# An output projection whose last slot hands over its two token halves one after the other

## The reference

```python
x = x + mixed @ w_out[l]                 # first block; then its mixture of experts
xn = rms_norm(x, ffn_norm[l])
...
h = h + mix                              # second block, layers 0 and 1; mix = o @ w_out
h = h + 0.5 * swiglu(rmsnorm(h, g[2]), ffn_w1[layer, 1], ffn_w3[layer, 1], ffn_w2[layer, 1])

def rmsnorm(x, g):
    xf = x.astype(F32)
    y = xf * lax.rsqrt(jnp.mean(xf * xf, axis=-1, keepdims=True) + EPS)
    return (y * g.astype(F32)).astype(x.dtype)
```

## Time and profile before

| | |
|---|---|
| median of 3 runs | 1673.91 us |
| the profiled execution's own time | 1673.79 us |
| its span in the trace | 1671.8 us |
| PE, DVE, ACT, POOL busy | 1554.4, 1140.2, 814.1, 42.5 us |
| mean granted clock of PE | 0.954 of full speed |

### The profile page before, as it was taken

How to read it: one execution, slowest core, us unless ns; L and a number is a source line. 1 busy time by engine, 2 the same in 40 slices (tenths; PEclk the granted TensorE clock), 3 DMA queues, 4 the chain that set the end, 5 groups by cost and what they waited for, 6 DMA issues and landing times.

```text
span 1671.8 us, 26989 instructions
## 1 busy us (share of the span) xinstructions
PE 1554.4 (93%) x9148; PEld 1352.5 (81%) x9148; DVE 1140.2 (68%) x1740; ACT 814.1 (49%) x1308; POOL 42.5 (3%) x53
## 2 busy tenths in 40 slices
PE   7898786999999989999996999999999999999997
PEld 6788674898898958888894788888788878888886
DVE  5845863798788947777544657777777765667775
ACT  6423442777677744444443453444444445654442
POOL 1120000000000000000000100000000000000000
PEclk9898787999999999999997599999999999999999
DMA  6312231799799947555451056556456544155552
GB/s 255 114 64 76 76 107 38 252 353 348 262 338 348 351 172 229 188 188 189 139 182 57 1 172 200 193 187 193 152 187 193 189 155 152 54 173 189 188 188 76
DMA packets 82148, 299.67 MB, mean 179 GB/s; under 512 B 9278, under 2 KB 9406, under 8 KB 81952
## 3 DMA queue, kind: packets, MB, share of 16 engines
q1 hardware_dynamic: 79632, 289.97, 51.6%
q0 software_dynamic: 2160, 8.66, 1.7%
q10 hardware_dynamic: 288, 0.12, 0.0%
HBM read 297.59 MB, written 1.11 MB: 179 GB/s over the span
## 4 chain that ended last, share of the span: by engine, by line
PE 85%; DVE 9%; ACT 4%; issue 1%; DMA 0%; POOL 0%; DVEq 0%; SPq 0%; POOLq 0%; ACTq 0%
PE ps L1680 17%; PE ps L1505 15%; PE ps L1506 14%; PE ps L1507 14%; PE ps L1678 10%; PE ps L1511 3%; PE ps L1677 2%; PE ps L1632 2%; DVE w_lo L921 2%; PE ps L1604 1%; PE ps L1697 1%; DVE xT L960 1%; PE ps L1772 1%; ACT arena L600 1%; ACT w_hi L545 1%
## 5 line engine op out<-in xcount | busy, mean ns | idle before, releaser
L921 DVE TENSOR_TENSOR w_lo<-raw,w_hi 128x1024 fp32r<-128x1024 f32 x549 | 653.4, 1221 | 230.7 <-ACT w_hi L545 229.5
L545 ACT ACTIVATE w_hi<-raw 128x1024 fp32r<-128x1024 f32 x549 | 549.1, 1055 | 337.6 <-PE ps L1507 306.4
L1680 PE MATMUL ps<-xT,w_hi 128*128 128x512 f32 x1232 | 439.6, 396 | 0.0
L1678 PE MATMUL ps<-xT,w_lo 128*128 128x256 f32 x1408 | 364.5, 279 | 0.0
L1678 PEld LDWEIGHTS ps<-xT,w_lo 128*128 128x128 f32 x1408 | 265.3, 188 | 16.1
L1680 PEld LDWEIGHTS ps<-xT,w_hi 128*128 128x128 f32 x1232 | 231.2, 188 | 47.1
L1505 PE MATMUL ps<-w_hi,xT 128*128 128x256 f32 (+2 forms) x848 | 261.6, 309 | 7.0 <-DVE w_lo L921 3.6
L1506 PE MATMUL ps<-w_lo,xT 128*128 128x256 f32 (+2 forms) x848 | 251.9, 297 | 0.0
L1507 PE MATMUL ps<-w_hi,xT 128*128 128x256 f32 (+2 forms) x848 | 251.8, 297 | 0.0
L1505 PE MATMUL ps<-w_hi,h_hi 128*128 128x512 f32 x480 | 188.4, 392 | 4.4 <-DVE h_lo L1121 4.4
L1506 PE MATMUL ps<-w_lo,h_hi 128*128 128x512 f32 x480 | 187.7, 391 | 0.0
(11 more groups left out here) (315 smaller groups left out, 1630.0 us busy)
## 6 DMA issues: line engine op xcount, KB each, us to landing
raw<-in_wstream SPq DMA_DIRECT2D x549, 512.0 KB, 5.0
arena<-bias_rows POOLq DMA_DIRECT2D x2, 2048.0 KB, 12.2
const<-in_const POOLq DMA_DIRECT2D x1, 1112.0 KB, 7.5
x_res<-in_x SPq DMA_DIRECT2D x2, 512.0 KB, 4.5
arena<-in_mem POOLq DMA_DIRECT2D x1, 1024.0 KB, 5.3
out<-arena SPq DMA_DIRECT2D x2, 512.0 KB, 2.7
smallw<-in_smallw POOLq DMA_DIRECT2D x1, 768.0 KB, 4.4
prow<-in_prow POOLq DMA_DIRECT2D x1, 512.0 KB, 5.1
```

Source lines behind the costliest of these rows:

```text
L545: nc.scalar.activation(w_hi[:, slot, lo:hi], raw[:, slot, lo:hi], ACT.Copy).then_inc(S_(f"hi_{part_}"), 1)
L921: tt(w_lo[:, slot, lo:hi], raw[:, slot, lo:hi], w_hi[:, slot, lo:hi].bitcast(F32), ALU.subtract).then_inc(S_(f"lo_{part_}"), 1)
L1678: low = mm(bank[:, 0:S], w_lo[:, s, c:c + P], xT_hi[:, k, :], start=False, stop=False)
L1680: last = mm(bank, w_hi[:, s, c:c + P], both, start=False, stop=k == KD - 1)
```

## The change

In the last slot of each of the three projections, the last matmul of token half 0 signals `half_psum`. DVE adds this half as soon as it comes, and signals `half_added`; ACT's Square of half 0 waits for that. Half 1 keeps its old signals. `RESIDUAL_ENDS` names the three slots that follow such a projection.

```diff
+RESIDUAL_ENDS = (MOE0, FFB0, FFD0)
...
                         if c:
-                            act.wait_ge(S_(wait[0]), wait[1] + t if wait[0] == "y_added" else wait[1])
+                            if wait[0] == "evacuated" and not t:
+                                act.wait_ge(S_("half_added"), RESIDUAL_ENDS.index(wait[2]) + 1)
+                            else:
+                                act.wait_ge(S_(wait[0]), wait[1] + t if wait[0] == "y_added" else wait[1])
...
-            norm(3, ("evacuated", evac_until(MOE0 - 1)))
+            norm(3, ("evacuated", evac_until(MOE0 - 1), MOE0))
...
                 if residual:
-                    dve.wait_ge(S_("d_used"), n + 1)
                     pair, n_first, places = psum_places(n)
                     w = len(places) * P
                     c = places[0][1][2]
                     for t in range(T):
+                        if n + 1 in RESIDUAL_ENDS and not t:
+                            end = RESIDUAL_ENDS.index(n + 1) + 1
+                            dve.wait_ge(S_("half_psum"), end)
+                        else:
+                            dve.wait_ge(S_("d_used"), n + 1)
                         ins = tt(x_res[:, t, c:c + w], ps[:, pair + t, 0:w], x_res[:, t, c:c + w], ALU.add)
+                        if n + 1 in RESIDUAL_ENDS and not t:
+                            ins.then_inc(S_("half_added"), 1)
                     ins.then_inc(S_("evacuated"), 1)
...
                         last = mm3(o, st, mv, k == 0, k == KD - 1)
+                    if not i and n + 1 in RESIDUAL_ENDS:
+                        last[2].then_inc(S_("half_psum"), 1)
```

More of the change, by code:

```diff
@@ L881, in _ @@
                 proj(n, evacuate=False)
-            norm(7, ("evacuated", evac_until(FFB0 - 1)))
+            norm(7, ("evacuated", evac_until(FFB0 - 1), FFB0))
             feed_forward(*ffs[2])
@@ L893, in _ @@
                 proj(n, evacuate=False)
-            norm(11, ("evacuated", evac_until(FFD0 - 1)))
+            norm(11, ("evacuated", evac_until(FFD0 - 1), FFD0))
             feed_forward(*ffs[4])
```

## The result

The changed kernel takes 1690.24 us (median of 4 runs, 1689.77 to 1691.09), the kernel before, run beside it, 1673.71 (4 runs, 1673.17 to 1674.88). The ratio is 1.0094 [1.0082, 1.0107]: 16.5 us slower. The forecast of 1669.7 us was wrong. What happened is the rival that I gave 0.04, and it is larger than I priced it. The profiled execution took 1691.09 us, its span 1689.1, and PE's mean granted clock is 0.935 (0.954 before).

What follows compares the result with a forecast made beforehand. PE was taken as the bound, except where it waits for the norms' serial chain. The profiled 1673.79 us less 4.21 gave 1669.6, and 0.1 for the median made 1669.7 us; range 1667.8 to 1672.8.

Steps and rivals of the forecast that it cites:

- the rival that I gave 0.04: Last attention, before place 3: falls to PE's lower clock; with 14 us fallen, +6.0 us net, 1679.9 us; chance 0.04.
- The sum: Norms behind the three projections: first add and first Square leave the chain, 1.41, 1.40 and 1.40 us, 4.21 in all.
- The signals and the read of the neighbouring bank: Three places: new PE signals taken as 0, at most 0.36 us; slower PSUM read 0, at most 0.1 each.
- The room to hide: Each place: hidden add and Square finish before the second Square is due, with 0.2, 0.2 and 0.25 us left.
- a shift's mean cost is nothing: Clock rise in the router's gather: monitor runs free of the program, so a shift has no side and costs nothing on average.
- The smaller rival: Router after place 1: clock rise stays while the gather comes earlier, 0.7 us lost, 1670.4; case put at 1671.3; chance 0.10.
- the clock's gain: Router's gather after place 1: an earlier clock rise gives back half of 3.0 us, 1668.2 us; chance 0.08.

Runs made afterwards that it cites:

- Runs 9 to 11: Useless matmuls ahead of the last attention: six in the changed kernel, 1673.01 us; nine in the kernel before, 1694.6; fifteen in the kernel before, 1678.2.
- run 5: Kernel before with the new signals at place 2 alone (FFB0): median 1690.88 us, ratio 1.0072.
- run 6: Kernel before with the new signals at place 1 alone (MOE0): 1674.08 us, ratio 0.9999.
- run 1: The changed kernel timed again, unchanged, against the kernel before: 1689.0 us, ratio 1.0089.
- run 8: Changed kernel with filler matmuls in the last attention's opening gaps and 8 more at its end: 1672.01 us, ratio 0.9989.
- run 9: Changed kernel with six useless matmuls behind the first slot of the projection feeding the last attention: 1673.01 us, ratio 0.9989.
- run 7: Kernel before with the new signals at places 1 and 3 only (MOE0, FFD0): 1672.3 us, ratio 0.999.

## Why the prediction was wrong

**The sum was right.** It had 1.41 + 1.40 + 1.40 = 4.21 us, and the timeline has 1.43 + 1.35 + 1.43 = 4.21. The signals and the read of the neighbouring bank cost nothing that shows. From the first filler to the next layer's first matmul it was 988.78 to 997.02, 8.24 us, and is 990.79 to 997.70, 6.91, at place 2. What failed is the step from that sum to the time, which took everything else as unchanged.

**The room to hide was right in size and tight where I said.** I gave 0.2 to 0.25 us. At place 2 the third split waited 0.31 us for ACT's copy, and that for a load, so the first add came later, and the second Square starts straight behind the first at 991.56, with no idle time of its own: the cover was 0.08 us too short there and 1.35 came in place of 1.43. As I had it, each tenth beyond the room costs a tenth.

**The step that failed is an argument against a rival.** I wrote of the last attention's fall: "Against: the clock was 1.00 with PE busy 9.97 of 10, and what comes before it keeps its own order and lengths. 0.04." Both halves failed.
- The window I took, 1430 to 1440, is the dense middle of the stage. The fall begins in its opening, 1412 to 1419, where PE was busy for 5.09 of 7 us already in the kernel before. I never looked at that window. A busy middle then doesn't bring the clock back: PE was busy for 45.71 of 47 us at 0.50. The earlier trace rows showed that much, at 940 to 950: the attention before place 2 ran at 0.50 with PE busy for 9.60 of 10.
- I took kept order and kept lengths for kept clock. Runs 9 to 11 show that the position decides, with order and lengths of the attention untouched: useless matmuls 28 us ahead of it turn 1690 into 1673 us, 1674 into 1695, and with six more of them, 1678.

**Two sizes of that rival were off.** I wrote that the stage starts 2.8 us earlier; what counts is 1.4 us, place 2's (run 5 against run 6). And I let 14 us of the stage fall, for 10.2 us. It was work of 29.8 us at the upper level, 47.8 at the lower, for 18.05 us. The price is 18.05/29.8 = 0.61 us for each microsecond, where I had 0.73, so the rate was a little too high and the length was half of what it should have been. 14 was a guess in the middle of the attention; that the clock stays down to about the attention's end could have been read from the attention before place 2, which stayed down from 905 to 960.

**On the clock's freedom.** Run 5 gives 1673 to 1675 us in two executions and 1690 or more in six. The rule of the Trainium skill that I weighed ("TensorE: Matmul & The Clock Gate", Part 1: the monitor runs free of the program) agrees with that, and so do the clock's edges, which keep their distances of 669.0 and 890.9 us whatever the program does. What I drew from it, that a shift's mean cost is nothing, doesn't hold here: the changed kernel went the same way in all of eight executions. The edges do not move with the program, but the program comes to place 2 at nearly one position against them, within 0.4 us.

**The smaller rival did not come as I had it.** I gave 0.7 us for a rise in the router that stays where it is while the gather comes 1.4 us earlier. In the changed kernel's first profile gather and rise kept their distance (1.83 and 1.86 us later, both), and in run 1, with place 1's norm 1.5 us earlier against the rise, the gain was gone before the gather started. So the clock can take all of place 1's gain and not half. Run 6 is 0.3 us below before, with an interval from -1.8 to +1.3 us, and from the rise near 960 to the last norm its profile has 705.25 us, before 705.24: nothing of place 1's 1.4 us is seen to reach the end.

**A slip in the range.** Its lower end, 1667.8, is called the clock's gain, which I had priced at 1668.2. Nothing hangs on it.

## What to carry to other kernels

Before work is moved in a kernel whose PE has idle stretches, list each place where the granted clock changes and each opening where PE has gaps although the clock holds; there the kernel stands on an edge, and a shift of 1.4 us at a distance of hundreds may cost ten times what was gained. Fill those gaps first, then judge the change with the fillers in both kernels (here 2.7 to 3.5 us faster, against 16.5 us slower without). A change that saves locally exactly what was planned and yet is slower in total should be tried with a small useless delay ahead of the stage that lost.

Three versions lie below the kernel before by about 0.1%, with intervals that just exclude 1: the change with fillers (run 8, 1672.01 us), the change with a delay of six matmuls (run 9, 1673.01), and places 1 and 3 alone (run 7, 1672.3). Of these only run 8 takes away the gaps; the others keep them and their edge.

## What the runs showed of the hardware

- A stage may run wholly at 1.2 GHz with PE busy for 45.71 of 47 us, and the same stage at 2.4 GHz with PE busy for 44.08 of 47. The clock held or was lost within its first 4 us.
- Whether gaps of the same size (5.09 and 5.15 of 7 us busy) bring the clock down depends on when they come: distances of 454.2 to 454.4 and of 457.6 us from the rise near 960 did, 455.6 to 456.0 and 459.4 did not. With the gaps filled (6.88 of 7 us busy) 454.2 did not either.
- The clock's edges kept their distances to each other in all 14 profiles: 669.0 us between the rises near 291 and 960, 890.9 between those near 69 and 960, 457.4 from the latter to the fall in four profiles. The program's instants moved against them by 2.8 us at place 1 and by 0.4 at place 2.
- Matmuls that came 1.41 us earlier took 8.77 us in place of 7.08, because the clock fell during them (0.66 over 263 to 268 in run 1).
- Eleven filler matmuls, or a delay of 1.3 us, were worth 15 to 17 us.
- The same program can take both ways: six executions of eight in run 5.
